# Modulation columns by multiply-and-sum on VectorE, with another placing of pieces, first choice and last rows

## What is computed

```python
cond = silu(c)
for i in range(4):
    shift, scale, gate = split(cond @ w_mod[i] + b_mod[i], 3)   # w_mod[i]: 1024 x 3072
    h = rms_norm(x, norm_pre_g[i]) * (1 + scale) + shift
    o = (gla, sgu, fox, gla)[i](h)
    x = x + gate * rms_norm(o, norm_post_g[i])
x = x + hybrid(x)
# expert layer, per row and head (8): scores to two sets of 128 keys, the best 16 of each,
# the best 16 of their 256 sums; out = sum softmax * gelu(u . down[e]) * up[e]
```

## Time and profile before

| | us |
|---|---|
| median of 3 runs | 1748.75 (1738.15 to 1750.39) |
| the profiled execution | 1739.41 |
| its span | 1737.6 |
| PE busy | 1393.7 (80%) |
| DVE busy | 1047.5 (60%) |
| ACT busy | 433.1 |
| POOL busy | 490.7 |
| moved by DMA | 591.53 MB, mean 340 GB/s |

### The profile page before, as it was taken

One profiled execution on the slowest core, in us unless ns is written; L12 is line 12 of the kernel. 1 busy time (PEld: TensorE's weight loads), 2 busy tenths in 40 slices (PEclk: granted clock), 3 DMA queues, 4 the chain that ended last, 5 costly groups with the idle time before them and its releaser, 6 DMA issues. The chain is left out here.

```text
span 1737.6 us, 13867 instructions
## 1 busy us (share of the span) xinstructions
PE 1393.7 (80%) x4158; PEld 717.6 (41%) x4158; DVE 1047.5 (60%) x2197; ACT 433.1 (25%) x974; POOL 490.7 (28%) x498
## 2 busy tenths in 40 slices
PE   6998988978999999999777777699787647666665
PEld 6454435444444455444354343455333312222222
DVE  3645554553233222313797998788866778877876
ACT  1221413423423421102133232132002221111111
POOL 2101210210000000000445546355344545444441
PEclk9998998989999999999897888798888878898898
DMA  9978884978556776887999989999999999999995
GB/s 386 377 256 303 312 340 171 347 282 295 213 207 219 277 265 242 290 293 265 402 361 357 413 339 403 412 400 413 410 414 414 348 412 422 421 422 421 422 421 248
DMA packets 108941, 591.53 MB, mean 340 GB/s; under 512 B 12450, under 2 KB 12706, under 8 KB 60612
## 3 DMA queue, kind: packets, MB, share of 16 engines
q0 software_dynamic: 67776, 312.56, 45.4%
q1 hardware_dynamic: 41092, 278.10, 42.2%
HBM read 589.55 MB, written 1.05 MB: 340 GB/s over the span
## 5 line engine op out<-in xcount | busy, mean ns | idle before, releaser
L948 PE MATMUL bank<-ring,hT 128*128 128x512 f32 x1888 | 866.6, 615 | 39.6 <-DVE room L1920 12.1
L948 PEld LDWEIGHTS bank<-ring,hT 128*128 128x128 f32 x1888 | 366.5, 198 | 482.2 <-issue 449.8
L877 POOL DMA_INDIRECT room<-in_peer_down,idx x92 | 102.5, 1114 | 525.1 <-DVE idx L1781 401.8
L1798 DVE CUSTOM_DVE_ANT_0 room<-room 128x1024 f32<-128x1024 f32 x180 | 218.6, 1221 | 50.6 <-DMA room<-in_pair,idx 38.4
L1203 PE MATMUL bank<-room 128*128 128x512 f32 x284 | 150.9, 676 | 96.5 <-ACT room L1493 94.2
L1813 DVE SCALAR_TENSOR_TENSOR x<-room,pcoef,x 128x1024 f32<-128x1024 f32 x121 | 155.7, 1287 | 28.0 <-DMA room<-in_peer_up,idx 27.5
L877 POOL DMA_INDIRECT room<-in_peer_up,idx x104 | 114.0, 1096 | 88.6 <-DVE pa L1798 42.3
L1203 PEld LDWEIGHTS bank<-room 128*128 128x128 f32 x284 | 57.5, 215 | 190.8 <-issue 97.2
L849 POOL DMA_DIRECT2D room<-in_w_mod x80 | 42.2, 528 | 326.3 <-DVE room L1567 206.5
L877 POOL DMA_INDIRECT room<-in_pair,idx x88 | 97.0, 1102 | 108.5 <-PE bank L1203 50.6
L927 PE MATMUL bank<-cst,room 128*128 128x128 f32 x424 | 64.7, 297 | 55.3 <-ACT room L1439 24.1
(11 more groups left out here) (304 smaller groups left out, 1527.4 us busy)
## 6 DMA issues: line engine op xcount, KB each, us to landing
ring<-in_wpk SPq DMA_DIRECT2D x248, 1024.0 KB, 7.0
room<-in_w_mod POOLq DMA_DIRECT2D x80, 512.0 KB, 8.2
room<-in_w_mod SPq DMA_DIRECT2D x8, 1024.0 KB, 15.8
room<-in_norm_post_g POOLq DMA_DIRECT2D x4, 512.0 KB, 5.0
rowb<-in_gate_bias SPq DMA_DIRECT2D x4, 512.0 KB, 9.0
room<-in_peer_up,idx POOLq DMA_INDIRECT x104, 12.5
room<-in_peer_down,idx POOLq DMA_INDIRECT x92, 12.4
room<-in_pair,idx POOLq DMA_INDIRECT x88, 14.3
```

The costliest lines, as they stand in the source:

```text
L877: return pool.indirect_dma_start(out=dst, out_offset=None, in_=A[table][0] if table != "pair" else A[table], in_offset=bass.IndirectOffset ...
L948: last = mm(bank[p][:, :], lhs, ring[:, h % 4, k * N:(k + 1) * N], start=(kk == 0), stop=(h == halves[-1] and k == 3))
L1798: v.tensor_tensor_reduce(out=row, in0=row, in1=u_(g // MINE), scale=1.0, scalar=0.0, op0=ALU.mult, op1=ALU.add, accum_out=pa[:, g // TOPK ...
```

## The change

Shift and scale: the host packs w_mod transposed for these two thirds, so that a piece is 128 finished outputs by all 1024 inputs. DVE multiplies it by silu(c), broadcast to all partitions (`crow`), and sums along the row: one instruction gives one finished column of `modr`. `mod_columns` adds the bias columns and forms 1 + scale times norm_pre_g. PE has no part in shift and scale any more, and its six pieces are DVE's. Pieces alternate shift and scale. The gate goes as before, with one sum per layer. There are six slots instead of four. Steps "mod" are placed two or three per block, and more in a gap behind an output block (5, 4, 2); mod_cols stands right ahead of the norm_in of its layer. In the expert layer tile 0's first choice and score steps come one block earlier, the choice has fewer and joined instructions, and the last eight up rows are added two per tick.

```diff
-for _name, _n in (("cond", 8), ("npre", 32), ...
+for _name, _n in (("cond", 8), ("bmod", 64), ("npre", 32), ...
...
+def pack_modulation(inputs):
+    pieces = []
+    for w in inputs["w_mod"]:
+        for j in range(KC):
+            pieces += [w[:, third * D + j * P:third * D + (j + 1) * P].T for third in range(2)]
+        pieces += [w[:, 2 * D:].reshape(P, KC, D)[:, k] for k in range(KC)]
+    return np.stack(pieces)
...
-            b(0, name="query", pre=[("norm_in", t, 5)]),
-            b(1, [("score_T", t, 0)], name="query"),
-            b(2, [("score_S", t, 0), ("score_T", t, 1)], name="query"),
+            b(0, [] if t else [("score_T", t, 0)], name="query", pre=[("norm_in", t, 5)]),
+            b(1, [("score_T", t, 0)] if t else [("score_S", t, 0)], name="query"),
+            b(2, ([("score_S", t, 0)] if t else []) + [("score_T", t, 1)], name="query"),
...
-TICKS = PICKS + REST + LEAD[1]
-PIECES = [(L, third, k) for L in range(DEPTH) for third in range(3) for k in range(KC)]
-PE_PIECES = (5, 7, 9, 11, 13, 15)
+TICKS = PICKS + REST + 2
+PIECES = [piece for L in range(DEPTH) for piece in
+          [(L, third, j) for j in range(KC) for third in range(2)] + [(L, 2, k) for k in range(KC)]]
+SLOTS = 6
...
-    return u < 7 * TOPK or u % 4 == 3 or (u % 2 and (u < MINE or u >= PICKS - 8))
+    return u < 7 * TOPK or (u % 4 == 3 and u < PICKS - 4) or (u % 2 and u < MINE) \
+        or u >= PICKS - 2 or (u % 2 and PICKS - 8 <= u < PICKS - 4)
...
 def added_at(v):
+    if v >= PICKS - 8:
+        return tick_of(PICKS - 2) + (v - PICKS + 8) // 2
     return tick_of(v) + LEAD[v // MINE]
...
-GROUPS = [(hh * TOPK, TOPK) for hh in range(PH)] + [(MINE + 4 * m, 4) for m in range(MINE // 4)]
+GROUPS = [(hh * TOPK, TOPK) for hh in range(PH)] + [(MINE + 4 * m, 4) for m in range(MINE // 4 - 1)] \
+    + [(PICKS - 4, 2), (PICKS - 2, 2)]
...
-    if mm[2] == "in0":
-        return (4, 4, 3, 2, 2, 2)[mm[3]]
-    return 4 + mm[3] if mm[2] == "out0" else 3
+PIECES_AT = {"in0": (3, 3, 3, 2, 2, 2), "out0": (3, 2), "in1": (3, 3, 3, 3, 3, 2), "out1": (3, 2),
+             "in2": (3, 3, 3, 3, 3, 3, 2, 2), "out2": (3, 2)}
+PIECES_IN_GAP = {"out0": 5, "out1": 4, "out2": 2}
...
+                if last in PIECES_IN_GAP and i == 0:
+                    add_pieces([PIECES_IN_GAP[last]])
...
+        if mm and mm[2] in ("in1", "in2", "in3") and mm[3] == 0:
+            order.append(("mod_cols", int(mm[2][2])))
         order += pre
...
-        if mm and mm[2] in ("out0", "out1", "out2") and mm[3] == 1:
-            order.append(("mod_cols", int(mm[2][3]) + 1))
...
-            if name == "query" and n == 2:
+            if name == "query" and n == 1:
                 order.append(("choose", 0))
-                rows.tick()
-            if name == "query" and n == 3:
-                rows.tick()
-                rows.tick()
+            if name == "query" and n >= 2:
+                for _ in range(n - 1):
+                    rows.tick()
...
-        mring = [at(M0 + i * D, D) for i in range(4)]
+        mring = [at(M0 + i * D, D) for i in (0, 1, 2, 3, 5)] + [at(KTC, D)]
+        crow = at(M0 + 4 * D, D)
...
+            load(crow, A["c"].to_broadcast([P, D]), "first_in")
...
             def fetch(n):
-                pool.wait_ge(S("summed"), summed_before(2 * KC if n < 2 * KC + 4 else n - 3))
+                pool.wait_ge(S("summed"), max(n - SLOTS + 1, 2 * KC - 4))
...
+            af(crow, crow, ACT.Silu).then_inc(S("cond"), 1)
...
             def add_piece(n):
...
+                if third < 2:
+                    v.tensor_tensor_reduce(out=piece, in0=piece, in1=crow, scale=1.0, scalar=0.0, op0=ALU.mult, op1=ALU.add,
+                                           accum_out=modr[:, L, third, k:k + 1]).then_inc(S("summed"), 1)
+                    return
...
+            def mod_columns(L):
+                dve.wait_ge(S("summed"), columns_of(L))
+                link(v.tensor_tensor(modc[:, L, :, :], modr[:, L, :, :],
+                                     const("bmod", 2 * KC * L, 2 * KC).rearrange("p (a b) -> p a b", a=2), ALU.add))
+                v.scalar_tensor_tensor(out=modc[:, L, 1, :], in0=modc[:, L, 1, :], scalar=1.0,
+                                       in1=const("npre", L * KC, KC), op0=ALU.add, op1=ALU.mult).then_inc(S("modc"), 1)
...
-                    v.tensor_copy(pixf[:, :, :], pix[:, :, :])
...
-                    link(v.tensor_copy(pabf[:, :, :], pab[:, :, :]))
...
+                    both = [P, 2, TOPK, TOPK]
+                    link(v.tensor_tensor(hot, const("iota").unsqueeze(1).unsqueeze(1).to_broadcast(both),
+                                         pab[:, :, :].unsqueeze(3).to_broadcast(both), ALU.is_equal))
+                    link(v.tensor_tensor(hot, hot, pix[:, :, :].unsqueeze(2).to_broadcast(both), ALU.mult))
...
+                    link(v.tensor_reduce(psel[:, :, :], hot, X, ALU.add))
...
-                    v.tensor_copy(idx[:, w, :], pidf[:, :]).then_inc(S("picked"), 1)
+                    v.scalar_tensor_tensor(out=idx[:, w, :], in0=psel[:, 0, :], scalar=float(NK), in1=psel[:, 1, :],
+                                           op0=ALU.mult, op1=ALU.add).then_inc(S("picked"), 1)
```

More of the change, by code:

```diff
@@ L272 @@
 DVE_NTH = {u: i for i, u in enumerate(ON_DVE)}
-ADDS = {added_at(v): [v] for v in range(PICKS)}
+ADDS = {k: [v for v in range(PICKS) if added_at(v) == k] for k in range(TICKS)}
 def adds_of(k):
-    return ADDS.get(k, [])
+    return ADDS[k]
 def sums_at(hh):
@@ L367, in make_order, with add_pieces @@
             second.append(c)
-    done, pending, ahead, piece = 0, [], False, 2 * KC
+    done, pending, ahead, last = 0, [], False, None
+    pieces = iter(range(2 * KC, len(PIECES)))
+    def add_pieces(counts):
+        for _ in range(sum(counts)):
+            order.append(("mod", next(pieces)))
     for c in first:
         if c in ("gap", "gap twice"):
-            for _ in range(len(c.split())):
+            for i in range(len(c.split())):
                 order += pending + ([] if ahead else second[done][0]) + [second[done][1]]
@@ L379, in make_order @@
             order.append(mm)
[L380 to L383, removed]
-        if mm and mm[2] in ("out0", "out1", "out2") and mm[3] == 1:
-            order.append(("mod_cols", int(mm[2][3]) + 1))
+        if mm:
+            last = mm[2]
+            add_pieces(PIECES_AT.get(last, ())[mm[3]:mm[3] + 1])
         if mm and not pending and not ahead:
@@ L854, in start_sums @@
                     pool.wait_ge(S(f"pd{p}"), n // 2 + 1)
[L855 to L858 removed]
+                link(nc.gpsimd.memset(gsum[L % 2], 0.0))
+                pool.dma_start(gsum[L % 2][0:1, :], A["b_mod"][L:L + 1, 2 * D:3 * D]).then_inc(S(f"gsum_init{L % 2}"), 16)
             def fetch_post(L):
@@ L978, in quad_values @@
                 return h_v(t, (n - 4) // 2)[:, head * DH:(head + 1) * DH]
-            def piece_columns(n, p):
-                _, third, k = PIECES[n]
-                pe.wait_ge(S(early_in(n // 2)), 16)
-                for j in range(KC):
-                    mm(bank[p][:, third * KC + j:third * KC + j + 1], early[n // 2][:, n % 2, j * P:(j + 1) * P],
-                       const("cond", k, 1), start=n == PE_PIECES[0] and j == 0, stop=False, skip_group_check=True)
-            pe.wait_ge(S("first_in"), 16)
+            pe.wait_ge(S("first_in"), 32)
             pe.wait_ge(S("ones_set"), 1)
             pe.wait_ge(S("pool_order"), 1)
-            pe.wait_ge(S("cond"), 1)
-            for piece in PE_PIECES[:2]:
-                piece_columns(piece, use("mod_cols", 0)[1])
             for step in ORDER:
@@ L997, in _ @@
                 a, b, c = WORK[t] if t < T else (None,) * 3
-                if kind == "mod_cols":
-                    L = t
-                    n, p = use(*step)
-                    if n >= 2:
-                        pe.wait_ge(S(f"ev{p}"), n // 2)
-                    if L == 0:
-                        for piece in PE_PIECES[2:]:
-                            piece_columns(piece, p)
-                    pe.wait_ge(S(f"sums_init{L % 2}"), sums_set(L))
-                    for j in range(2 * KC):
-                        if j % KC == 0:
-                            pe.wait_ge(S("summed"), summed_before(L * 3 * KC + j + KC))
-                        last = mm(bank[p][:, j:j + 1], sums[L % 2][j // KC][:, (j % KC) * P:(j % KC + 1) * P],
-                                  ones[:, 0:1], start=L > 0, stop=True, skip_group_check=L == 0)
-                    last.then_inc(S(f"pd{p}"), 1)
-                elif kind == "mod_gate":
+                if kind == "mod_gate":
                     L, i = t, step[2]
```

119 lines of the change are left out of this document (47 added, 72 removed).

## The result

The changed kernel takes 1697.2 us (four runs, 1693.06 to 1698.97), the kernel before 1747.44 (four runs, 1738.15 to 1750.39): a ratio of 0.974, 95% interval 0.972 to 0.977 (the ratio on record; the two medians alone would give 0.971). The profiled execution after took 1697.2 with a span of 1695.4; against the profiled 1739.41 before that is 42.2 us less, where the prediction summed 33.6.

A forecast was written before the change was run, and what follows sets the result against it. PE was taken to bound the kernel up to about 830 us, DMA after that. Terms summing to 33.6 us came off the profiled 1739.4, and 9.3 was added for the median: 1715, range 1697 to 1742.

The forecast's parts named there:

- b: Behind out0: PE's one-column products and its wait for L1920 with the slower block behind it go; 10 us gained.
- g: First choice one block earlier: row fetches can start 8 us earlier, only six of them move; 5 us gained.
- a: The start: DVE takes all sixteen first pieces, PE's first projection starts at 38.1 instead of 47.79; 8.7 us gained.
- j: Crowding in the first 100 us: more bytes and slots, weights share the DMA engines with pieces; 4 us taken off.
- h: Shorter choices: about 0.7 us of DVE per choice saved, mostly where DVE waits anyway; 1 us gained.
- i: The end: fewer additions between the last row's multiply-and-sum and the final additions; 2 us gained.
- c: The gate in in1: one piece fewer ahead and two more slots filled shorten waits for late pieces; 4 us gained.
- d: Behind out1: the products' 3.63 us go, the chain with PE's 3.13 us wait for L1920 moves up; 3.4 us gained.
- e: Behind out2: L1920 comes 1.3 us earlier with two pieces ahead, PE's products become a wait; 1.5 us gained.
- f: in2: POOL's wait behind the norm_post_g load stays, only one piece fewer stands behind it; 2 us gained.
- crowding: Rival, chance 0.18: pieces and weights pulled forward collide, a, c and f bring nothing; 17 us gained, 1732.
- All waits go: Rival, chance 0.14: six slots end every DVE wait for a piece, the clock stays up; 52.7 us gained, 1696.

The follow-up runs named there:

- run 1: Changed kernel, with the small product with wlow waiting only for its own two loads instead of all five constant loads; 1695.56 us, ratio 0.972 to the kernel before.
- run 2: run 1's kernel, with the loads of sgu_ln_g and sgu_ln_b (1 MB) issued later, behind the first out block; 1694.16 us, ratio 0.972 to the kernel before.
- run 3: run 2's kernel, with the pieces of in0 placed later (1, 1, 2, 2, 2, 3 and two per gap); 1687.26 us, ratio 0.967 to the kernel before.
- run 4: Changed kernel, with a dummy turn in the shared PSUM banks put back behind the second out block of layers 0 to 2; 1703.25 us, ratio 0.977.
- run 5: Kernel before, with only the turn removed: columns of layers 1 to 3 formed in another bank, products kept; 1734.33 us against 1745.85, ratio 0.991.
- run 6: Changed kernel, with six slots kept but only four pieces fetched ahead; 1708.06 us, ratio 0.979 to the kernel before.
- run 11: run 3's kernel, with the norm_post_g load moved half a layer of pieces later in POOL's queue; 1681.37 us, ratio 0.965 to the kernel before.
- run 8: Changed kernel, with the first choice and tile 0's score steps back where they stood before; 1700.71 us, ratio 0.975 to the kernel before.
- run 9: Changed kernel, with the choice's separate instructions of before (three conversions more, pairs not joined); 1699.17 us, ratio 0.975 to the kernel before.
- run 10: Changed kernel, with the old tail: the last eight up rows added one per tick; 1700.77 us, ratio 0.976 to the kernel before.
- run 7: Changed kernel, with pieces placed as before and columns formed right behind the out blocks, without a turn; 1697.09 us, ratio 0.973.

## Why the prediction was right, and where it was not

The direction was right and the size near: 1715 was forecast, 1697 to 1742 as the range, and 1697.2 lies 0.2 us inside its lower edge, which is luck (one of the four executions took 1693.06). Of the 17.8 us, 8.6 are gain that the sum missed (42.2 against 33.6), and 9.3 are the term that I added for the median, since the profiled execution before was near its fastest; the one after is at its median, so the median moved by 50.2 and the profile by 42.2. By its parts the sum was less right than by its total, because errors cancelled: b to g gave 21.1 us more than forecast, a and j together 4.5 less, h and i 1.3 less, and the expert layer took 6.6 back.

- **a, the start, 8.7 forecast, 0.2 measured.** The working on DVE was right: block at 37.0 (forecast 38.1; a piece takes 1.15 us one behind the other, not 1.30). The 1.0 taken off for the clock was more than needed: the first block took 8.72 us, 0.2 more than before. The step that failed is "PE starts at 38.1, 9.7 us earlier" taken as the gain. It looked at the first block only. The next step waits for all five constants, and behind it stood the weights (run 1). The price of j, 4 us for crowding, was set for this region, so a and j together were to give 4.7 and gave 0.2 at the tenth block. Runs 1 to 3 show the cause: the loads, not DVE's pieces, set when the blocks behind the first can start.
- **b, 10 forecast, 11.2 measured.** Right in size; the products (4.1) and the wait with its slower block (7.3) went. The reason given for the wait was half: L1920 was late behind a piece, but without the turn PE would not have had to wait for it at all (runs 4 and 5).
- **c, 4 forecast, 7.9 measured.** Undersized. The mechanism is mostly the one named, slots: with four ahead 6.5 us are lost between out0 and this place (run 6). I took half of an interval whose upper end was the truth. The other 1.4 us have no run of their own.
- **d, e, 3.4 and 1.5 forecast, 9.3 and 7.1 measured.** This is the step that failed in kind. I wrote that PE's products at out2 "become a wait" and that at out1 the 3.13 us stay, because I took the dependence on L1920 for given. It hung on the turn, which the change removed together with the products. The diff shows it in one word, `mod_cols` in the line that hands out the banks; my cut of the diff did not even have that line. Run 4 prices it at 2.4 us at out1, run 5 at 2.8; the products were 3.6, and slots bring 1 (run 6). Some 2 of the 9.3 at out1 stay open. At out2 run 4 gives 4.0 and run 5 1.8, beside 3.6 for the products.
- **f, 2 forecast, 5.0 measured.** The wait in POOL's queue stays as predicted and even grew, from 17.20 to 27.02 us. With four pieces ahead it is 18.24 (run 6), so the two more slots lengthen it. The place that the prediction looked at brought the 2 us forecast. What it did not look at is the slower block and the late gate piece ahead of it, most of the rest; no run separates the two. Run 11 shows that the wait in the queue still costs some 5.6 us.
- **g, 5 forecast, 6.5 at its place.** Right: 3.5 to 4.9 at the end (run 8).
- **h, 1 forecast.** Right: 2 by the medians with a spread larger than that (run 9).
- **i, 2 forecast, 1.7 measured** (run 10).
- **"Nothing can take the gain back" from 450 to 820 us**: true but for some 2 us, it is 40.0 to 40.6 up to 787 us and not under 38.7 until 830. But the sentence in "what would show it wrong", an end that moves less than the first fetch, did come: 47.2 at the fetch, 42.2 at the end. The expert layer gave back 6.6 us between its beginning and the last rows.

The rivals: crowding was real, at the start only; its sum of 17 also leaves out g and h without a reason. "All waits go" lies within 2 us of the result at 1696, but by another sum, with 8.7 from the start that didn't come, and with 3.4 and 1.5 for d and e as in the forecast, whose waits did go. DVE didn't hold the start, and no column made late held up PE by more than 0.6 us: behind the three gaps PE waits 1.19, 1.19 and 1.79 us for norm_in (L1853), where it waited 1.22, 1.18 and 1.19 before. That it would not matter where the columns are made (run 7) no rival said.

## What to carry to other kernels

When an edit removes a user of a shared, alternating buffer, follow the whole chain of turns: the users behind it change their partner, and a wait can vanish, or appear, without any instruction becoming faster. When a step of one engine moves earlier, look at the next two waits behind it before counting it as gain: one semaphore for five loads makes the smallest one's landing the price of all, and behind that stands the bandwidth. And when the last stage is bound by transfers, time the start of that stage: what was gained before it arrived at the end nearly whole here, and what was gained within it on another engine mostly did not.

## What the runs showed of the hardware

A load of 1 KB took 26.8 us from issue to landing behind some megabytes in the same queue, in a stretch (30 to 57 us) in which DMA was at 1.02. Taking 1 MB out of the first 60 us moved the later blocks by 5.4 us in one execution each, twice what its bytes take at 420 GB/s. The multiply-and-sum of 128x1024 with its result read behind it repeats every 1.15 us, less than the 1.22 and 0.08 of its two rows added. The low product (L1040) after the idle 10.74 us took 3.60 us and after 1.04 us of waiting (run 1) 1.92. The windows give the granted clock (the third number from the end), first of run 1 at its first block, then of the changed kernel around its idle time:

```profile
37.00:47.00 10.00, 9.54 (x16) 3.90 (x16) 4.01 (x4) 3.21 (x10) 1.50 (x3) 0.74 1.02 407
46.00:60.00 14.00, 3.52 (x16) 2.23 (x16) 0.00 (x0) 0.38 (x1) 0.53 (x1) 0.66 1.03 409
```

Both means lie between the two levels, so PE was at 1.2 GHz for part of each. The first block, too, is slower by the clock, as the prediction had it: 9.54 us in run 1 at 0.74, after 9.34 us of standing still. In the changed kernel the view gives 1.00 for the same place, but there the trace's records of the clock begin only at 40.28 us, and what lies before a record counts as full. The weight loads of that block show the change of level at that time, 0.34 us before it and 0.19 after:

```profile
39.71 0.34 PEld L972 LDWEIGHTS bank<-ring,hT 128*128 128x128 f32 x1 [0.52 <-issue]
40.43 0.19 PEld L972 LDWEIGHTS bank<-ring,hT 128*128 128x128 f32 x1 [0.38 <-issue]
```
